# Weights of the experts, projections and feed-forward layers stored in DRAM piece by piece, one 8 KB run a partition

## The chip, the cores and the metric

The kernel runs on one core of a Trainium2 chip. The metric is the device time of one execution in microseconds; the kernel before takes 2042.43 us (median of 3 runs, 2041.69 to 2044.41).

## What is computed

Two blocks of two layers each, over 256 tokens of width 1024, all in f32. Cut to what matters for the weights:

```python
# first block, layer 0 (even mixer) and layer 1 (odd mixer)
mod = silu(c) @ ada_w[layer] + ada_b[layer]              # 1024 x 6144
h = rms_norm(x) * (1 + sc1) + sh1
x = x + g1 * mixer(h, w_in, w_out)                       # 1024 x 3584 or 3072, 1024 x 1024
h = rms_norm(x) * (1 + sc2) + sh2
for e in range(16):                                      # top 2 of 16 experts, from the best of 4 groups
    he = silu(h @ w_gate[e]) * (h @ w_up[e])             # 1024 x 512 each
    y += combine[:, e] * (he @ w_down[e])                # 512 x 1024
x = x + g2 * y
# second block, layer 0 (rwkv) and layer 1 (dilated attention)
x = x + 0.5 * swiglu_ffn(x, pre_w_in, pre_w_out)         # 1024 x 5632, 2816 x 1024
x = x + mixer(rms_norm(x), ...)                          # a_w_in 1024 x 2816, a_w_out; b_w_q, b_w_out, kv_w
x = x + 0.5 * swiglu_ffn(x, post_w_in, post_w_out)
```

Every weight is used once, by all 256 tokens. The experts' weights are 2 x 16 x 3 matrices of 2 MB, 201 MB in all, and are read whole, whatever the router picks.

## The kernel before, in words

Five engines run one program each, written out by hand with semaphores; SP's (`sp`, lines 746 to 810) does little but issue the loads of weights, in the order of the list `PL.pieces` that the class `Plan` (lines 142 to 245) makes before the program is built.

**Pieces.** A piece is 128 partitions x 2048 f32, 8 KB a partition, 1.05 MB. Outside the expert stages the pieces go through `ring`, three slots of one piece; a slot's next load waits for the events in `after`, mostly the split of the piece that it held before. The split makes two parts of each piece, `w_hi` by ScalarE (`split_piece`, L2344) and `w_lo` by VectorE (L3112), and TensorE multiplies by both. `static_piece(n)` issues piece n:
- kind `ada`: layer 0's `ada_w`, 24 pieces, a partition's 8 KB being one run of DRAM already (row `8 p + t` of the matrix), runs 192 KB apart. Unchanged.
- kind `gemm`: a projection, 61 pieces. `(k p) n -> p k n` gives partition p the rows p, 128 + p, ... of the matrix: 8 runs of 1 KB (pieces of 256 columns, 19 of them: `a_in` and the first 4 column groups of `odd_in`) or 4 runs of 2 KB (512 columns, 42).
- kinds `gate`, `up`, `down`: a feed-forward piece, 132 in all. Gate and up are 8 runs of 1 KB, 256 columns wide; down is 2 runs of 4 KB.
- kind `rwkv`: parameters. Unchanged.
- kind `moe`: a whole expert stage, `moe(name, blocks)`.

**The expert stages.** `experts` holds twelve pieces, in three thirds. A stage has 24 passes: 8 of gate (k = rows 128 k to 128 k + 127 of all 16 experts), 8 of up, 8 of down (2 halves of the columns x 4 parts of the rows). A pass is 4 pieces, one for each 4 experts (`load_block(p, g)`, issued at L796): 4 runs of 2 KB a partition, one from each expert. In gate and up weights a run of one partition is followed in memory by that of the next partition; in down weights, which are 4 KB wide, runs of neighbouring partitions lie 4 KB apart. The first twelve pieces are issued as their places come free at the end of the stage before; from pass 3 on a piece waits for `m_base` (TensorE is done with the same piece of three passes before), and the first of a pass also for `m_dve` and `m_act` (the copies are done too).

TensorE (`group(p, g)`, L1616) multiplies for each pass 4 base groups (their own weights from `experts`, one piece each) and 4 further groups, whose 15 tiles VectorE (L3552) and ScalarE (L2550) copy out of `experts` by the router's choice. Between passes stand turned tiles (`turn`, L1623; `slot_weights` and `turned_sel`, L1571 and L1580), the next layer's modulation (L1324, L1328), and the sums over experts (`scatter`, L1631).

**POOL's loads** (`block.gpsimd`) run beside SP's on a queue of their own: at the start the inputs and `mem_w_kv` (`mem_weights`, L837), later layer 1's `ada_w` (`ada_load_pair`, L904, and `ada_load`, L899), which VectorE multiplies and sums (L3240) and TensorE in part (L1490), and small tables. `ada_load_pair` takes two neighbouring parts of a row, 8 KB a partition; `ada_load` one, 4 KB. None of them is changed.

```python
def load_block(p, g):                                    # in moe(name, blocks)
    ...
    at = 512 * (NE * third(layer, p) + 4 * g)
    sp.dma_start(experts[:, at:at + 4 * 512].rearrange("p (e n) -> p e n", e=4), src.rearrange("e p n -> p e n"))\
      .then_inc(sem(pass_landed(layer, p, g)[0]), 16)
```

Of the kernel before, what the change touches and what calls it, by code (L numbers as in the profile page):

```python
# [30 lines left out]
P = 128  # L31
# [3 lines left out]
KD = D // P  # L35
# [4 lines left out]
PIECE = 2048  # L40
# [9 lines left out]
DFF = 2816  # L50
HC = 256
MOE_PASSES = 24
MOE_DEPTH = 3
BASE_GROUPS, GROUPS = 4, 8
# [169 lines left out]
def plan():  # L224
    p = Plan()

    for row in range(KD):
        p.ada(row, 0)
    p.gemm("even_in", EVEN_W, between=EVEN_ADA)
    p.gemm("even_out", D)  # L230
    p.moe("moe0")
    p.gemm("odd_in", ODD_W, feat=range(4))
    p.gemm("odd_out", D)
    p.moe("moe1")
    p.swiglu("pre0", FFN_CHUNKS)
    p.gemm("a_in", A_W, feat=range(5))
    p.rwkv()
    p.gemm("a_out", D)
    p.swiglu("post0", FFN_CHUNKS)
    p.gemm("kv", 1536)  # L240
    p.swiglu("pre1", FFN_CHUNKS)
    p.gemm("b_q", D)
    p.gemm("b_out", D, deep=4)
    p.swiglu("post1", FFN_CHUNKS)
    return p


PL = plan()
STAGES = {**PL.gemms, **PL.swi}

# [52 lines left out]
def build(nc, a, out):  # L303
    ctx = ExitStack()
    with ctx:
        def sb(name, shape, dt=F32):
            return ctx.enter_context(nc.sbuf_tensor(name, shape, dt))
# [3 lines left out]
        def sem(name):  # L311
            if name not in sems:
                sems[name] = ctx.enter_context(nc.semaphore(name))
            return sems[name]
# [15 lines left out]
        x = sb("x", [P, NT, D])  # L330
# [9 lines left out]
        router_w = sb("router_w", [P, KD, NE])  # L340
        router_b = sb("router_b", [P, NE])
        order_i = sb("order_i", [P, OVER_TILES + 1], I32)

        def overlay(name, shape, dt, at):

            return nc.alloc_sbuf_tensor_at(name, shape, dt, offset=at)

        experts = overlay("experts", [P, MOE_DEPTH * NE * 512], F32, pool_at + 4 * (PROJ + 1024))
# [14 lines left out]
        def view(off, *dims):  # L363
            n = int(np.prod(dims))
            v = pool[:, off:off + n]
            if len(dims) == 2:
                return v.rearrange("p (a b) -> p a b", a=dims[0])
            if len(dims) == 3:
                return v.rearrange("p (a b c) -> p a b c", a=dims[0], b=dims[1])
            return v  # L370
# [14 lines left out]
        def piece(n):  # L385

            s = PL.pieces[n]["slot"]
            return ring[:, s * PIECE:(s + 1) * PIECE]
# [122 lines left out]
        def third(layer, p):  # L511
            return (p + 1 - layer) % MOE_DEPTH
# [35 lines left out]
        def kind_of(p):  # L548
            return ("gate", p) if p < 8 else ("up", p - 8) if p < 16 else ("down", p - 16)
# [8 lines left out]
        def pass_landed(layer, p, g):  # L558
            return f"m_landed{p % MOE_DEPTH}{g}", 16 * (MOE_PASSES // MOE_DEPTH * layer + p // MOE_DEPTH + 1)
# [42 lines left out]
        gate = view(HT, NT, 768)  # L602
# [112 lines left out]
        for name, g in PL.gemms.items():  # L715
            for c in range(g["n"]):
                kind = gemm_dst(name, c)[0]
# [28 lines left out]

        @block.sync
        def _(sp):
            def source(kind, name, c):

                layer = int(name[-1])
                w_in = a[f"ffn_{name[:-1]}_w_in_2"][layer].rearrange("(k p) n -> p k n", p=P)
                w_out = a[f"ffn_{name[:-1]}_w_out_2"][layer].rearrange("(k p) n -> p k n", p=P)
                return {"gate": w_in[:, :, HC * c:HC * c + HC], "up": w_in[:, :, DFF + HC * c:DFF + HC * c + HC],
                        "down": w_out[:, 2 * c:2 * c + 2, :]}[kind]

            def load(n, src, k):
                s = PL.pieces[n]["slot"]
                sp.dma_start(piece(n).rearrange("p (k n) -> p k n", k=k), src).then_inc(sem(f"landed{s}"), 16)

            def static_piece(n):
                pc = PL.pieces[n]
                kind, what = pc["kind"], pc["what"]
                for e in pc["after"]:
                    sp.wait_ge(sem(e[0]), e[1])
                if kind == "ada":
                    src = a["ada_w"][0].rearrange("(p t) n -> p (t n)", t=KD)
                    load(n, src[:, what * PIECE:(what + 1) * PIECE].unsqueeze(1), 1)
                elif kind == "gemm":
                    name, o, cols, k0, ks = what  # L770
                    src = {"even_in": a["even_w_in"][0], "even_out": a["even_w_out"][0], "odd_in": a["odd_w_in"][0],
                           "odd_out": a["odd_w_out"][0], "a_in": a["a_w_in_2"][0], "a_out": a["a_w_out_2"][0], "kv": a["kv_w_2"],
                           "b_q": a["b_w_q_2"][0], "b_out": a["b_w_out_2"][0]}[name]
                    load(n, src.rearrange("(k p) n -> p k n", p=P)[:, k0:k0 + ks, o:o + cols], ks)
                elif kind == "rwkv":
                    for o, src in ((3072, a["c_rw_masks"]), (1536, a["a_lnx_g_2"][0].partition_broadcast(P)),
                                   (2304, a["a_lnx_b_2"][0].partition_broadcast(P))):
                        sp.dma_start(rwkv_par[:, o:o + src.shape[1]], src).then_inc(sem("rwkv_in"), 16)
                else:
                    name, c = what  # L780
                    load(n, source(kind, name, c), 2 if kind == "down" else KD)

            def moe(name, blocks):

                layer = int(name[-1])
                def load_block(p, g):

                    kind, k = kind_of(p)
                    es = slice(4 * g, 4 * g + 4)
                    if kind == "down":  # L790
                        h, f = k // 4, k % 4
                        src = a["exp_w_down"][layer, es, P * f:P * f + P, 512 * h:512 * h + 512]
                    else:
                        src = a["exp_w_gate" if kind == "gate" else "exp_w_up"][layer, es, P * k:P * k + P, :]
                    at = 512 * (NE * third(layer, p) + 4 * g)
                    sp.dma_start(experts[:, at:at + 4 * 512].rearrange("p (e n) -> p e n", e=4), src.rearrange("e p n -> p e n"))\  # L796
                      .then_inc(sem(pass_landed(layer, p, g)[0]), 16)

                order = [(p, g) for p in range(MOE_DEPTH) for g in range(BASE_GROUPS)]
                if layer == 0:  # L800
                    order[8:12] = [(2, 3), (2, 0), (2, 1), (2, 2)]
                for p, g in order:
                    block = BASE_GROUPS * third(layer, p) + g
                    if block >= 3:
                        for e in blocks[block - 3]:
                            sp.wait_ge(sem(e[0]), e[1])
                    elif layer == 0:
                        sp.wait_ge(sem("ada1_used"), (12, 14, 16)[block])
                    elif block == 0:
                        sp.wait_ge(sem("sb_pv"), 16)  # L810
                    load_block(p, g)
                for p in range(MOE_DEPTH, MOE_PASSES):
                    n = MOE_PASSES * layer + p
                    for g in range(BASE_GROUPS):
                        sp.wait_ge(sem("m_base"), BASE_GROUPS * (n - MOE_DEPTH) + g + 1)
                        if g == 0:
                            sp.wait_ge(sem("m_dve"), len(DVE_TILES) * (n - MOE_DEPTH + 1))
                            sp.wait_ge(sem("m_act"), len(ACT_TILES) * (n - MOE_DEPTH + 1))
                        load_block(p, g)

            for n, pc in enumerate(PL.pieces):
                if pc["kind"] == "moe":
                    moe(pc["what"], pc["after"])
                else:
                    static_piece(n)
            sp.wait_ge(sem("x_new"), 10)
            sp.dma_start(out.rearrange("a (t p) d -> p (a t) d", p=P), x[:, :, :]).then_inc(sem("stored"), 16)
            sp.wait_ge(sem("stored"), 16)
# [175 lines left out]
        TR_BASE, n = {}, 0  # L1004
# [1868 lines left out]
        def _(dve):  # L2873
# [1061 lines left out]
            swiglu("post1")  # L3935


_WEIGHTS = ["x", "c", "ada_w", "ada_b", "even_w_in", "even_w_out", "odd_w_in", "odd_w_out", "router_w", "exp_w_gate",
            "exp_w_up", "exp_w_down", "mem_2", "ffn_pre_w_in_2", "ffn_pre_w_out_2", "ffn_post_w_in_2",
            "ffn_post_w_out_2", "mem_w_kv_2", "a_w_in_2", "a_w_up_2", "a_a_up_2", "a_g_up_2", "a_w_out_2", "b_w_q_2",  # L3940
            "b_w_out_2", "kv_w_2", "rel_bias_2", "a_lnx_g_2", "a_lnx_b_2", "router_b"]


# [33 lines left out]
```

## Time and profile before

| what | value |
|---|---|
| median of 3 runs | 2042.43 us (2041.69 to 2044.41) |
| profiled execution, first to last instruction | 2041.6 us |
| TensorE, VectorE, ScalarE busy | 1897.6, 1175.1, 943.9 us |
| bytes read from DRAM | 472.17 MB, 232 GB/s over the span |
| first issue of an `experts` load of the first expert stage | 192.6 us |
| last issue of an `experts` load of the second expert stage | 891.4 us |

The profiled execution's own time isn't given apart from its span, which is 0.8 us under the median of the runs.

How to read it: the page cuts the span into 40 slices of 51 us and gives for each the busy share of every engine and of the 16 DMA engines, with the rate in GB/s. A window is the same for any stretch: for each engine the busy time in us with its number of instructions in brackets, then TensorE's granted clock, the DMA engines' share, and GB/s. The share of the DMA engines can pass 1, since one engine's packets overlap a little.

### The profile page before, as it was taken

How to read it: one execution, taken by the hardware profiler on the slowest of the kernel's cores; microseconds unless marked ns; L12 is line 12 of the kernel's file. 1: busy time of each engine (PE TensorE's matmuls, PEld its weight loads, DVE VectorE, ACT ScalarE, POOL GpSimd, SP SyncE). 2: the span in 40 equal slices, each digit the busy share in tenths (PEclk: the TensorE clock that was granted, in tenths of full speed). 3: DMA queues.
4: the chain of work that ended last, by engine and by line, in shares of the span. 5: the costliest groups of instructions: out<-in, count | busy, mean ns of one | idle time of the engine just before them, and what ended most of it. 6: DMA issues, size and time to landing. Idle time of an engine off the chain costs nothing.

```text
span 2041.6 us, 32610 instructions
## 1 busy us (share of the span) xinstructions
PE 1897.6 (93%) x13784; PEld 1381.8 (68%) x13784; DVE 1175.1 (58%) x1636; ACT 943.9 (46%) x1347; POOL 77.4 (4%) x132
## 2 busy tenths in 40 slices
PE   6998988798998988889999998899999999999998
PEld 4787523244976332338888987788887888778887
DVE  5778633444877432447556664665556675636565
ACT  4345445345463543455445733354445444445442
POOL 2031000000010000000000000000000000200000
PEclk9999999989999989899999989999999999999999
DMA  9887999998958899995555410255555555605552
GB/s 357 320 263 264 333 387 386 387 368 292 344 164 318 310 387 387 371 339 196 186 189 178 127 44 4 85 185 188 195 179 175 192 195 186 171 1 191 195 192 104
DMA packets 261218, 476.43 MB, mean 233 GB/s; under 512 B 8513, under 2 KB 118145, under 8 KB 255697
## 3 DMA queue, kind: packets, MB, share of 16 engines
q1 hardware_dynamic: 250960, 431.02, 60.6%
q0 software_dynamic: 10112, 43.32, 6.4%
q8 instruction: 110, 1.80, 0.4%
q14 instruction: 36, 0.29, 0.0%
HBM read 472.17 MB, written 2.14 MB: 232 GB/s over the span
## 4 chain that ended last, share of the span: by engine, by line
PE 73%; DMA 12%; DVE 7%; ACT 5%; issue 2%; SPq 0%; POOL 0%; ACTq 0%; DVEq 0%; POOLq 0%
PE psum L1175 16%; PE psum L1210 11%; PE psum L1616 9%; PE psum L1180 8%; PE psum L1130 6%; DMA experts<-in_exp_w_down 4%; DMA experts<-in_exp_w_up 4%; DMA experts<-in_exp_w_gate 2%; PE psum L1558 1%; PE psum L1344 1%; PE psum L1079 1%; PE psum L1143 1%; PE psum L1145 1%; PE psum L1144 1%; DVE w_lo L3112 1%
## 5 line engine op out<-in xcount | busy, mean ns | idle before, releaser
L3112 DVE TENSOR_TENSOR w_lo<-ring,w_hi 128x2048 fp32r<-128x2048 f32 x191 | 436.0, 2289 | 192.2 <-ACT w_hi L2344 190.4
L2344 ACT ACTIVATE w_hi<-ring 128x2048 fp32r<-128x2048 f32 x191 | 364.7, 1913 | 207.0 <-PE psum L1210 118.1
L1175 PE MATMUL psum<-h_both,w_hi 128*128 128x512 f32 x1408 | 442.6, 395 | 1.9 <-DVE h_both L3894 1.3
L1180 PEld LDWEIGHTS psum<-h_both,w_lo 128*128 128x128 f32 x1408 | 264.5, 188 | 61.8
L2550 ACT ACTIVATE pool<-experts 128x512 f32 x332 | 184.0, 621 | 228.1 <-PE psum L1616 98.0
L3552 DVE COPY pool<-experts 128x512 f32 x380 | 140.9, 423 | 245.2 <-PE psum L1616 115.4
L1180 PE MATMUL psum<-h_both,w_lo 128*128 128x256 f32 x1408 | 277.3, 278 | 0.0
L1175 PEld LDWEIGHTS psum<-h_both,w_hi 128*128 128x128 f32 x1408 | 217.4, 189 | 5.7 <-issue 1.7
L2376 ACT ACTIVATE pool<-psum 128x512 f32<-128x512 f32 x88 | 52.6, 598 | 254.6 <-PE psum L1180 254.5
L1616 PE MATMUL psum<-pool 128*32 128x512 f32 x1008 | 128.4, 626 | 12.5 <-DVE pool L3552 8.5
L1616 PE MATMUL psum<-experts,pool 128*32 128x512 f32 x1024 | 122.3, 607 | 15.7 <-DMA experts<-in_exp_w_down 12.9
L1616 PEld LDWEIGHTS psum<-pool 128*32 128x32 f32 x1008 | 32.6, 112 | 100.9 <-DVE pool L3552 66.3
L1210 PE MATMUL psum<-w_hi,hid_hi 128*128 128x512 f32 x320 | 98.9, 390 | 0.0
L1210 PE MATMUL psum<-w_lo,hid_hi 128*128 128x512 f32 x320 | 98.5, 389 | 0.0
L1210 PE MATMUL psum<-w_hi,hid_lo 128*128 128x512 f32 x320 | 98.5, 389 | 0.0
L1130 PE MATMUL psum<-w_hi,h_both 128*128 128x512 f32 x352 | 98.0, 400 | 0.0
L1616 PEld LDWEIGHTS psum<-experts,pool 128*32 128x32 f32 x1024 | 35.1, 111 | 90.4 <-issue 64.6
L1616 PE MATMUL psum<-experts,xg_high 128*32 128x512 f32 x512 | 63.4, 603 | 23.4 <-DMA experts<-in_exp_w_up 14.9
L1616 PE MATMUL psum<-pool,xg_high 128*32 128x512 f32 x512 | 70.4, 652 | 13.0 <-ACT pool L2550 11.5
L1130 PEld LDWEIGHTS psum<-w_hi,h_both 128*128 128x128 f32 x352 | 65.5, 188 | 17.2 <-issue 4.0
L1143 PE MATMUL psum<-w_hi,h_both 128*128 128x512 f32 x160 | 65.9, 412 | 8.4 <-DVE w_lo L3112 5.7
L3150 DVE TENSOR_TENSOR pool<-pool,psum 128x512 f32<-128x512 f32 x44 | 30.2, 687 | 69.7 <-ACT pool L2376 69.7
(507 smaller groups left out, 2998.6 us busy)
## 6 DMA issues: line engine op xcount, KB each, us to landing
experts<-in_exp_w_gate SPq DMA_DIRECT2D x64, 1024.0 KB, 12.1
experts<-in_exp_w_up SPq DMA_DIRECT2D x64, 1024.0 KB, 14.4
experts<-in_exp_w_down SPq DMA_DIRECT2D x64, 1024.0 KB, 15.0
ring<-in_ffn_pre_w_in SPq DMA_DIRECT2D x44, 1024.0 KB, 5.1
ring<-in_ffn_post_w_in SPq DMA_DIRECT2D x44, 1024.0 KB, 5.2
ring<-in_ada_w SPq DMA_DIRECT2D x24, 1024.0 KB, 7.0
ring<-in_ffn_pre_w_out SPq DMA_DIRECT2D x22, 1024.0 KB, 4.9
ring<-in_ffn_post_w_out SPq DMA_DIRECT2D x22, 1024.0 KB, 4.9
```

The source lines that it names most:

```text
L1130: m = pe.matmul(bank(pair + t)[:, lo:lo + cols], left[:, d, P * t:P * t + P], right[:, k, :], start=first, stop=last)
L1143: pe.matmul(dst, h_hi[:, d, ts], wh[:, k, :], start=d == 0, stop=False)
L1175: pe.matmul(bank(4 + 2 * j + f).rearrange("p (s n) -> p s n", s=2), wh[:, k, P * f:P * f + P], h_both[:, :, k, :], start=k == 0, stop=Fals ...
L1180: return pe.matmul(bank(4 + 2 * j + f)[:, 0:T], wl[:, k, P * f:P * f + P], h_hi[:, k, :], start=False, stop=k == KD - 1, skip_group_check= ...
L1210: m = pe.matmul(bank(2 * t + h), left[:, f, ts], right[:, f, 512 * h:512 * h + 512], start=first, stop=False)
L1616: m = pe.matmul(moe_bank(p, g)[own, :], x_, w, start=first, stop=last)
L2344: act.activation(w_hi[:, (s["split"] + r) % 3, :], piece(s["pieces"][r]), ACT.Copy)\
L2376: act.activation(out_, psum[:, b:b + 2, T:2 * T], ACT.Copy).then_inc(sem("low_moved"), 1)
L2550: act.activation(over_w(layer, p, i), experts[:, bass.ds(tile_at[i // 2] + 512 * NE * third(layer, p), 512)], ACT.Copy)\
L3112: dve.tensor_tensor(w_lo[:, slot, :], piece(s["pieces"][r]), w_hi[:, slot, :].bitcast(F32), ALU.subtract).then_inc(sem("w_lo"), 1)
L3150: dve.tensor_tensor(h, h, psum[:, 4:6, 0:T], ALU.add).then_inc(sem("hid_part"), 1)
L3552: dve.tensor_copy(over_w(layer, p, i), experts[:, bass.ds(tile_at[i // 2] + 512 * NE * third(layer, p), 512)])\
```

## The change

On the host, before the launch, the arrays are put in another order: `weight_pieces` has one 1 MB block for each of the 193 pieces of projections and feed-forward layers, `exp_blocks` one for each of the 192 expert pieces, and in a block the 8 KB of partition 0 come first, then those of partition 1, and so on. The loads read these blocks whole. Order, number and size of the loads, their waits, where they land and everything that the engines compute stay as they are.

```diff
+    p.streamed = [n for n, piece in enumerate(p.pieces) if piece["kind"] in ("gemm", "gate", "up", "down")]
...
-            def load(n, src, k):
+            def load(n, src):
                 s = PL.pieces[n]["slot"]
-                sp.dma_start(piece(n).rearrange("p (k n) -> p k n", k=k), src).then_inc(sem(f"landed{s}"), 16)
+                sp.dma_start(piece(n), src).then_inc(sem(f"landed{s}"), 16)
...
-                    load(n, src[:, what * PIECE:(what + 1) * PIECE].unsqueeze(1), 1)
-                elif kind == "gemm":
-                    name, o, cols, k0, ks = what
...
-                    load(n, src.rearrange("(k p) n -> p k n", p=P)[:, k0:k0 + ks, o:o + cols], ks)
+                    load(n, src[:, what * PIECE:(what + 1) * PIECE])
...
-                    name, c = what
-                    load(n, source(kind, name, c), 2 if kind == "down" else KD)
+                    load(n, a["weight_pieces"][PL.streamed.index(n)])
...
-                    if kind == "down":
-                        h, f = k // 4, k % 4
-                        src = a["exp_w_down"][layer, es, P * f:P * f + P, 512 * h:512 * h + 512]
-                    else:
-                        src = a["exp_w_gate" if kind == "gate" else "exp_w_up"][layer, es, P * k:P * k + P, :]
                     at = 512 * (NE * third(layer, p) + 4 * g)
-                    sp.dma_start(experts[:, at:at + 4 * 512].rearrange("p (e n) -> p e n", e=4), src.rearrange("e p n -> p e n"))\
+                    sp.dma_start(experts[:, at:at + 4 * 512], a["exp_blocks"][layer, p, g])\
                       .then_inc(sem(pass_landed(layer, p, g)[0]), 16)
...
+def expert_blocks(gate, up, down):
+
+    by_row = [w.reshape(2, BASE_GROUPS, 4, KD, P, 512).transpose(0, 3, 1, 4, 2, 5) for w in (gate, up)]
+    by_half = down.reshape(2, BASE_GROUPS, 4, 4, P, 2, 512).transpose(0, 5, 3, 1, 4, 2, 6)
+    return np.concatenate([w.reshape(2, 8, BASE_GROUPS, P, PIECE) for w in (*by_row, by_half)], 1)
+
+
+def weight_pieces(n):
+
...
+        pieces.append(rows.reshape(-1, P, rows.shape[1]).transpose(1, 0, 2).reshape(P, PIECE))
+    return np.stack(pieces)
```

## Rows read from the trace of the kernel before

**Rows 1.** The page: span, busy times, and DMA in 40 slices.

```profile
span 2041.6 us, 32610 instructions
...
PE 1897.6 (93%) x13784; PEld 1381.8 (68%) x13784; DVE 1175.1 (58%) x1636; ACT 943.9 (46%) x1347; POOL 77.4 (4%) x132
...
DMA  9887999998958899995555410255555555605552
GB/s 357 320 263 264 333 387 386 387 368 292 344 164 318 310 387 387 371 339 196 186 189 178 127 44 4 85 185 188 195 179 175 192 195 186 171 1 191 195 192 104
```

**Rows 2.** Window of a feed-forward stage: PE, PEld, DVE, ACT, POOL busy, clock, DMA share, GB/s.

```profile
1000.00:1050.00 50.00, 50.00 (x267) 42.89 (x266) 30.12 (x26) 21.95 (x19) 0.00 (x0) 1.00 0.58 191
```

**Rows 3.** Windows of the first (260 to 490) and second (700 to 910 us) expert stage.

```profile
260.00:400.00 140.00, 114.19 (x928) 36.28 (x920) 44.68 (x117) 58.16 (x106) 0.00 (x0) 0.95 1.05 386
400.00:460.00 60.00, 57.87 (x431) 25.65 (x432) 29.11 (x66) 27.22 (x50) 0.57 (x1) 0.91 1.04 370
460.00:490.00 30.00, 23.48 (x178) 7.36 (x173) 8.22 (x20) 12.50 (x24) 0.00 (x0) 0.94 1.04 369
700.00:820.00 120.00, 99.28 (x808) 33.82 (x804) 39.08 (x104) 52.32 (x95) 0.00 (x0) 0.94 1.05 387
820.00:840.00 20.00, 19.54 (x146) 7.00 (x149) 10.74 (x22) 7.70 (x14) 0.00 (x0) 0.87 1.03 363
840.00:860.00 20.00, 16.69 (x132) 3.96 (x128) 6.61 (x17) 8.95 (x16) 0.00 (x0) 0.91 1.04 370
860.00:880.00 20.00, 19.53 (x136) 8.66 (x132) 13.07 (x27) 11.55 (x22) 0.00 (x0) 1.00 1.05 383
880.00:910.00 30.00, 24.26 (x184) 7.03 (x176) 8.97 (x22) 12.98 (x25) 0.00 (x0) 0.94 1.03 358
```

**Rows 4.** Shorter windows inside the first expert stage.

```profile
290.00:310.00 20.00, 14.11 (x120) 3.38 (x120) 5.22 (x15) 6.30 (x12) 0.00 (x0) 1.00 1.05 386
340.00:350.00 10.00, 9.51 (x93) 3.18 (x86) 2.96 (x8) 3.86 (x7) 0.00 (x0) 1.00 1.05 387
435.00:440.00 5.00, 4.51 (x48) 1.45 (x44) 1.60 (x5) 2.27 (x4) 0.00 (x0) 1.00 0.98 318
```

**Rows 5.** The chain of waits, first expert stage: start us, us, what.

```profile
280.56 27.80 DMA experts<-in_exp_w_gate x2
```

**Rows 6.** The view of DMA: packets, then issues xcount, KB each, median us to landing.

```profile
DMA packets 261218, 476.43 MB, mean 233 GB/s; under 512 B 8513, under 2 KB 118145, under 8 KB 255697
...
ring<-in_ffn_pre_w_in SPq DMA_DIRECT2D x44, 1024.0 KB, 5.1
...
rcols<-in_rwkv_cols POOLq DMA_DIRECT2D x1, 25.0 KB, 30.6
```

**Rows 7.** POOL in order of time: start us, us, line, operation, xcount, idle before.

```profile
5.97 0.55 POOL L845 DMA_DIRECT2D rcols<-in_rwkv_cols  x1
...
186.03 2.09 POOL L904 DMA_DIRECT2D pool<-in_ada_w  x4 [2.89 <-DVE w_lo L3112]
```

**Rows 8.** Windows in which ada_w's 8 KB runs are fetched.

```profile
12.00:20.00 8.00, 2.27 (x5) 1.85 (x6) 4.57 (x6) 2.87 (x7) 0.21 (x1) 1.00 1.02 413
190.00:198.00 8.00, 7.61 (x34) 5.97 (x32) 7.46 (x10) 2.04 (x2) 0.00 (x0) 1.00 1.03 425
```

**Rows 9.** The chain of waits again, before the second expert stage.

```profile
608.82 3.74 DMA pool<-in_ada_w
...
626.50 6.65 DMA pool<-in_ada_w
```

**Rows 10.** TensorE in order of time: start us, us, line, operation, idle before.

```profile
38.34 1.88 PE L1344 MATMUL psum<-pool 128*128 128x512 f32 x4
...
227.07 1.06 PE L1490 MATMUL psum<-pool,cact 128*32 128x512 f32 x8 [0.41 <-DMA pool<-in_ada_w]
...
229.34 3.00 PE L1558 MATMUL psum<-sel,xn_parts 128*128 128x512 f32 x12 [0.57 <-DVE sel L3482]
```

More of the change, by code:

```diff
@@ L748, in _ @@
         def _(sp):
[L749 to L755, printed above, removed]
-            def load(n, src, k):
+            def load(n, src):
                 s = PL.pieces[n]["slot"]
-                sp.dma_start(piece(n).rearrange("p (k n) -> p k n", k=k), src).then_inc(sem(f"landed{s}"), 16)
+                sp.dma_start(piece(n), src).then_inc(sem(f"landed{s}"), 16)
             def static_piece(n):
@@ L767, in static_piece @@
                     src = a["ada_w"][0].rearrange("(p t) n -> p (t n)", t=KD)
-                    load(n, src[:, what * PIECE:(what + 1) * PIECE].unsqueeze(1), 1)
-                elif kind == "gemm":
-                    name, o, cols, k0, ks = what
-                    src = {"even_in": a["even_w_in"][0], "even_out": a["even_w_out"][0], "odd_in": a["odd_w_in"][0],
-                           "odd_out": a["odd_w_out"][0], "a_in": a["a_w_in_2"][0], "a_out": a["a_w_out_2"][0], "kv": a["kv_w_2"],
-                           "b_q": a["b_w_q_2"][0], "b_out": a["b_w_out_2"][0]}[name]
-                    load(n, src.rearrange("(k p) n -> p k n", p=P)[:, k0:k0 + ks, o:o + cols], ks)
+                    load(n, src[:, what * PIECE:(what + 1) * PIECE])
                 elif kind == "rwkv":
@@ L786, in load_block @@
                 def load_block(p, g):
-                    kind, k = kind_of(p)
-                    es = slice(4 * g, 4 * g + 4)
-                    if kind == "down":
-                        h, f = k // 4, k % 4
-                        src = a["exp_w_down"][layer, es, P * f:P * f + P, 512 * h:512 * h + 512]
-                    else:
-                        src = a["exp_w_gate" if kind == "gate" else "exp_w_up"][layer, es, P * k:P * k + P, :]
                     at = 512 * (NE * third(layer, p) + 4 * g)
-                    sp.dma_start(experts[:, at:at + 4 * 512].rearrange("p (e n) -> p e n", e=4), src.rearrange("e p n -> p e n"))\
+                    sp.dma_start(experts[:, at:at + 4 * 512], a["exp_blocks"][layer, p, g])\
                       .then_inc(sem(pass_landed(layer, p, g)[0]), 16)
@@ L3935, in _ @@
             swiglu("post1")
[L3938 to L3941, printed above, removed]
+def expert_blocks(gate, up, down):
[3 more added lines that the diff above has]
+def weight_pieces(n):
+    dense = {"even_in": n["even_w_in"][0], "even_out": n["even_w_out"][0], "odd_in": n["odd_w_in"][0], "odd_out": n["odd_w_out"][0],
+             "a_in": n["a_w_in_2"][0], "a_out": n["a_w_out_2"][0], "kv": n["kv_w_2"], "b_q": n["b_w_q_2"][0], "b_out": n["b_w_out_2"][0]}
+    pieces = []
+    for at in PL.streamed:
+        kind, what = PL.pieces[at]["kind"], PL.pieces[at]["what"]
+        if kind == "gemm":
+            name, o, cols, k0, ks = what
+            rows = dense[name][P * k0:P * (k0 + ks), o:o + cols]
+        else:
+            stage, c = what
+            layer, part = int(stage[-1]), f"ffn_{stage[:-1]}_w"
+            o = HC * c + (DFF if kind == "up" else 0)
+            rows = n[f"{part}_out_2"][layer][HC * c:HC * c + HC] if kind == "down" else n[f"{part}_in_2"][layer][:, o:o + HC]
+        pieces.append(rows.reshape(-1, P, rows.shape[1]).transpose(1, 0, 2).reshape(P, PIECE))
+    return np.stack(pieces)
+_WEIGHTS = ["x", "c", "ada_w", "ada_b", "router_w", "mem_2", "mem_w_kv_2", "a_w_up_2", "a_a_up_2", "a_g_up_2", "rel_bias_2",
+            "a_lnx_g_2", "a_lnx_b_2", "router_b"]
 def kernel(**inputs):
@@ L3967 @@
     arrays["rel_t"] = np.ascontiguousarray(np.concatenate([rel, np.zeros((256 - rel.shape[0], 8), rel.dtype)], 0))
+    arrays["weight_pieces"] = weight_pieces(n)
+    arrays["exp_blocks"] = expert_blocks(n["exp_w_gate"], n["exp_w_up"], n["exp_w_down"])
     arrays.update(constants())
```

## The prediction

> **What bounds the kernel now.** I read the page's slices first [rows 1]: TensorE is busy 93% of the span, and the DMA engines are full in two stretches only, slices 6 to 10 and 14 to 18, where they move up to 387 GB/s. These are the two expert stages. Next come windows. In a feed-forward stage [rows 2] TensorE is busy 50.00 of 50 us and DMA moves 191 GB/s; three feed-forward windows I read were alike to 2 GB/s. No faster transfer helps there. In the expert stages [rows 3] it is the other way round: DMA share 1.05, 386 and 387 GB/s over 140 and 120 us, while TensorE is busy 114.19 and 99.28 us. Inside them two kinds of window alternate [rows 4]: at 340 us TensorE is fed (9.51 of 10, 93 matmuls), at 290 us it starves (14.11 of 20, 120 matmuls). The chain of waits says the same: from 280.56 us it stands for 27.80 us in transfers of gate weights [rows 5]. A pass of 16 experts is 4 pieces of 1.05 MB, 10.8 us at 387 GB/s. Twelve pieces fit in the ring, some 32 us of transfer, so TensorE's side work (turns, sums) doesn't stop the stream. In the first two thirds of each stage the transfers alone set the pace.
>
> **What the change alters.** The same bytes go over the same queues into the same places, after the same waits. Only the runs in DRAM differ: 192 expert pieces in 2 KB runs, 132 feed-forward pieces (88 in 1 KB, 44 in 4 KB) and 61 of projections (19 in 1 KB, 42 in 2 KB) all become 128 runs of 8 KB. That is 240,640 packets replaced by 49,280; of the 261,218 packets of [rows 6] some 69,900 should be left. No engine gains or loses an instruction, and SP issues as many transfers.
>
> **The rate of 8 KB runs** isn't shown for these weights, but the stream has others. From 190 to 198 us POOL's four `ada_w` loads (8 KB a partition, [rows 7]) are nearly alone in the engines and go at 425 GB/s [rows 8]; from 12 to 20 us SP's `ada_w` pieces of 8 KB, mixed with POOL's small loads, go at 413. The bounds are 387 (nothing gained) and 425. I take 425: it is the row with least else in it, and a share of 1.03 beside 1.05 says that both are the engines at full work. A piece then takes 2.47 instead of 2.71 us.
>
> A rule speaks against this. The Trainium skill, page "DMA: Bandwidth & Descriptors", Specifications, gives 512 B as the smallest transfer for line rate; by it runs of 2 KB are there already and the sum is 0. The rows of 387 and 425 GB/s don't agree with it. The same page, "Why small descriptors are slow", gives some 3 cycles for each packet, 67 for 2 KB against 64 of data; an estimate from that is 3.4% for the expert stages, a third of what the rows show.
>
> **First two thirds of the expert stages.** 140 us at 386 GB/s are 54.0 MB, at 425 GB/s 127.2 us: 12.8 us saved. 120 us at 387 are 46.4 MB, 109.3 us: 10.7 saved. Ends: 413 GB/s saves 9.2 and 7.6.
>
> **The down thirds** (400 to 490, 820 to 910 us) need two sums [rows 3].
> - DMA: 33.3 and 33.1 MB. At 387 they would take 86.0 and 85.4 us, at 425 78.3 and 77.8: 7.7 and 7.6 saved by the rate. The rows take 90, since they hold short dips, as 318 GB/s at 435 us [rows 4], eight in all over both stages, and in down weights only. Down weights are the only expert loads whose 2 KB runs lie 4 KB apart, so the dips may well go with the layout: then 11.7 and 12.2 are saved.
> - TensorE: it can't go faster than fed. By busy time (81.35 us at 9.51 per 10) it needs 85.5 of the 90 us, and 84.1 in the second stage: caps of 4.5 and 5.9. By matmuls (93 per 10 us fed, 178 in the 30 starved us of the first stage; 132 and 184 in 50 us of the second) the caps are 10.9 and 16.0. A starved group's last matmul counts its whole length as busy, so the first pair is too low.
>
> The rate terms lie between the caps, and I take them. What the dips give back above that meets TensorE, which is what is late next. Sum of the four: 12.8 + 10.7 + 7.7 + 7.6 = 38.8 us.
>
> **Where the long packets cost.** SP's weights share the 16 engines with POOL's loads. If the queues take turns by packet, a POOL packet waits behind 8 KB instead of 2 KB. The nearest price: two equal loads of `ada_w` took 3.74 us alone and 6.65 beside SP's experts [rows 9]. The later one (512 KB, 8 packets an engine) gets 6 KB × 8 × 16 = 0.79 MB more in front, 1.85 us, and stands on the chain. At 227.07 us TensorE waits 0.41 us for a 1 MB `ada_w` load (again 8 packets an engine, 1.85 us), and had 0.57 us of slack behind it [rows 10]: 1.3 us. At the start the second half of `mem_w_kv` is in before `rcols`, which lands at 5.97 + 30.6 = 36.6 us [rows 6, 7], and TensorE reads it at 38.34 [rows 10]; SP has two pieces queued, and if both go in front, not only one's worth, that is 1.05 MB or 2.5 us more, so 39.1: 0.8 us late. Together 4.0 us, between 0 (SP has nothing queued) and 8. The Trainium skill, the same page, "Queues, rings and completion order", has the queues taking turns at packets; no row here shows the order of packets.
>
> **Costed at nothing.** The feed-forward and projection pieces: a 1 MB piece in 1 KB runs lands 5.1 us after its issue, and 191 GB/s are one piece of 1.05 MB every 5.5 us, by TensorE's pace and not by the transfers' [rows 2, 6], and if TensorE were not full, a piece would still gain only the few tenths between 2.5 us at 425 and its present transfer time. SP's issuing: behind the ring of three slots.
>
> **Sum.** The profiled execution spans 2041.6 us, 0.8 below the median 2042.43 of the runs. 2041.6 - 38.8 + 4.0 = 2006.8 us, and with the 0.8 around it 2007.6 us.
>
> **Rivals.**
> - *Packets cost less than the rows say* (the rate of 425 is partly POOL's queue or those addresses). At 400 GB/s the 166.8 MB of both stages save by rate 431.4 - 417.0 = 14.4 us (431.4 being the four rate-bound times at 386 and 387), less 4.0: 2032 us. For it: no 8 KB row is wholly alone. Against: 413 GB/s even when mixed. 5%. The skill's estimate above would end here.
> - *The engines are at their ceiling already* (share 1.05, TensorE 93% busy): only the turns cost, 2042.4 to 2046.4. Against it is the 425. 4%, half of it within 0.2%. The skill's 512 B rule ends here.
> - *Slower: lock step in memory.* Place: the expert stream. A piece is now one block of 1 MB in which the engines' runs lie at equal power-of-two distances; today's `ada_w` runs lie 192 KB apart and show no such block. The dips to 318 GB/s prove that addresses can slow the stream. Price: at 350 GB/s the 166.8 MB take 476.6 instead of 440 us (both stages whole), and 4.0 more: 2083 us. It decides from below 383 GB/s (166.8 MB in 436 us). Against: gate and up runs are adjacent already, without a dip. 3%. The skill's same page, "Latency and other measured facts", tells of such slowing for row pitches of 512 KiB and more, and recommends contiguous tiles; its pitches are not met here.
> - *The change doesn't do what it says*: if the engines cut 8 KB runs at 2 KB, packets stay at 261,000 and the time at 2042.4. Against: `ada_w` runs now. 2%.
>
> **How the numbers follow.** 0.2% (4.1 us) is what can be told from no change. My forecast has 86%. Low end: 425, dips gone, no cap, no turns lost: 2042.4 - 47.4 = 1995.0. High end: 413 with 9.2 + 7.6 + 4.5 + 5.3 = 26.6 saved and 4.0 lost: 2019.8, rounded to 2020. Nothing further is needed to leave out less than 2 in 10. Faster: 86 + 5 = 91%. Same: 2 + 2 = 4%. Slower: 2 + 3 = 5%.
>
> **What the profile after would show.** Packets near 69,900; windows of both expert stages at 420 to 425 GB/s until the down passes; the gap from the first to the last `experts` transfer shorter by 18 to 21 us in each stage; down passes with TensorE fed most of the time; feed-forward windows still at 50.00 of 50; the `ada_w` load near 626 us at 8 us or more. I am wrong if those windows stay at 387, if the dips grow, or if the chain shows a POOL transfer of over 10 us.

## The result, and the profile after

The changed kernel takes 2007.24 us (median of 4 runs, 2004.27 to 2009.94) against 2042.97 us of the kernel before in the same comparison: a ratio of 0.9824, 95% interval 0.9809 to 0.9839. The forecast was 2007.6 us, between 1995.0 and 2020. The profiled execution spans 2006.9 us, 34.7 less than the one before.

The page of the kernel after (lines as in [rows 1], and the packets of [rows 6]):

```profile
span 2006.9 us, 32610 instructions
...
PE 1879.5 (94%) x13784; PEld 1385.4 (69%) x13784; DVE 1175.4 (59%) x1636; ACT 943.7 (47%) x1347; POOL 77.6 (4%) x132
...
DMA  9885999997957799975555210345545555505552
GB/s 355 310 290 215 353 393 392 421 420 289 347 161 312 301 421 420 421 294 210 190 193 181 86 43 4 148 169 189 190 174 190 189 191 189 151 21 190 189 189 105
DMA packets 69857, 476.43 MB, mean 237 GB/s; under 512 B 8512, under 2 KB 8576, under 8 KB 15056
```

The same bytes, the same instructions, 69,857 packets instead of 261,218, and 421 GB/s where 387 stood. Windows of the kernel after, first in the gate and down passes of the first stage, one in the down passes of the second, then a feed-forward stage (columns as in [rows 2]):

```profile
280.00:290.00 10.00, 9.51 (x92) 3.24 (x88) 3.00 (x9) 3.84 (x8) 0.00 (x0) 1.00 1.02 421
430.00:440.00 10.00, 8.93 (x68) 3.90 (x64) 4.82 (x11) 5.42 (x10) 0.00 (x0) 1.00 1.01 421
850.00:860.00 10.00, 9.54 (x89) 3.05 (x92) 6.12 (x15) 6.62 (x14) 0.00 (x0) 1.00 1.01 415
1000.00:1050.00 50.00, 50.00 (x267) 42.90 (x266) 30.17 (x25) 21.71 (x18) 0.00 (x0) 1.00 0.54 190
```

The expert stream is faster in gate, up and down weights alike and has lost its dips; the feed-forward stage is as it was [rows 2], down to the number of matmuls.

To follow the time, I cut both executions at marks that the chain of waits has in every kernel: the start of the gather that opens an expert stage, the start of the last group of sums that closes it, and the feed-forward pieces. The chain of the kernel before, then of the kernel after (start us, us, what; x14 closes a stage, x32 opens the second; the first opens at 229.34 us before [rows 10]):

```profile
496.54 3.43 PE psum L1631 x14
...
658.61 7.52 PE psum L1558 x32
...
915.48 3.41 PE psum L1631 x14
```

```profile
5.19 34.32 DMA pool<-in_mem_w_kv
39.55 1.98 PE psum L1323 x4
...
221.96 10.39 DMA pool<-in_ada_w
234.09 14.54 PE psum L1537 x64
...
483.49 3.41 PE psum L1610 x14
...
613.48 8.01 DMA pool<-in_ada_w
...
648.17 9.14 PE psum L1537 x32
...
886.54 3.41 PE psum L1610 x14
```

The expert stages went from 267.2 to 249.4 us and from 256.9 to 238.4 us: 36.3 us saved. The rest nearly cancels: the start up to the first gather is 4.75 us longer, the stretch between the stages 2.6 us longer (162.1 to 164.7), and the rwkv stage, in which hardly a weight is loaded, 7.2 us shorter. Three of the forecast's places of cost are in the chain by name: POOL's `mem_w_kv`, and two `ada_w` loads.

### The profile page after: what moved, and what is told of

Same layout as the page of the kernel before. It is cut to its first block, busy times and chain, and to the rows that moved or that the text cites. A ratio compares the mean times of both kernels' runs of the same rounds, so it can differ in the third digit from the quotient of the medians.

```text
span 2006.9 us, 32610 instructions
## 1 busy us (share of the span) xinstructions
PE 1879.5 (94%) x13784; PEld 1385.4 (69%) x13784; DVE 1175.4 (59%) x1636; ACT 943.7 (47%) x1347; POOL 77.6 (4%) x132
## 2 busy tenths in 40 slices
DMA packets 69857, 476.43 MB, mean 237 GB/s; under 512 B 8512, under 2 KB 8576, under 8 KB 15056
## 4 chain that ended last, share of the span: by engine, by line
PE 75%; DMA 10%; DVE 7%; ACT 5%; issue 2%; SPq 0%; POOL 0%; DVEq 0%; ACTq 0%; POOLq 0%
PE psum L1154 16%; PE psum L1189 11%; PE psum L1595 10%; PE psum L1159 8%; DMA experts<-in_exp_blocks 7%; PE psum L1109 6%; DMA pool<-in_mem_w_kv 2%; PE psum L1537 2%; PE psum L1122 1%; PE psum L1610 1%; PE psum L1123 1%; PE psum L1124 1%; PE psum L1323 1%; DMA pool<-in_ada_w 1%; DVE w_lo L3091 1%
## 5 line engine op out<-in xcount | busy, mean ns | idle before, releaser
L1595 PE MATMUL psum<-pool 128*32 128x512 f32 x1008 | 123.1, 603 | 12.9 <-DVE pool L3531 10.9
L1595 PE MATMUL psum<-pool,xg_high 128*32 128x512 f32 x512 | 65.2, 612 | 13.9 <-ACT pool L2529 10.4
## 6 DMA issues: line engine op xcount, KB each, us to landing
pool<-in_mem_w_kv POOLq DMA_DIRECT2D x4, 1024.0 KB, 16.6
```

The source lines that it names most:

```text
L1595: m = pe.matmul(moe_bank(p, g)[own, :], x_, w, start=first, stop=last)
```

## The experiments

Eight more kernels ran, and the changed one once more (after_again). The medians are over all runs of a kernel, and the ratios against the kernel before run beside it; the stage lengths, between the marks above, are those of one profiled execution each:

| kernel | median us | first stage | between | second stage | rwkv |
|---|---|---|---|---|---|
| before | 2042.4 | 267.2 | 162.1 | 256.9 | 270.1 |
| after | 2007.2 | 249.4 | 164.7 | 238.4 | 262.9 |
| experts_only | 2006.2 | 249.2 | 164.6 | 238.4 | 265.0 |
| pieces_only | 2043.7 | 267.1 | 161.9 | 257.2 | 267.1 |
| blocks_2k | 2038.4 | 264.8 | 161.9 | 254.8 | 267.0 |
| blocks_4k | 2018.2 | 253.4 | 162.8 | 243.3 | 263.6 |
| down_old | 2023.9 | 256.5 | 164.7 | 248.4 | 262.3 |
| after_again | 2005.9 | 248.3 | 163.4 | 236.8 | 261.4 |
| short_beside | 2001.2 | 249.1 | 160.3 | 237.1 | 262.6 |
| mem_8k | 2007.3 | 245.5 | 163.1 | 236.8 | 262.5 |
| short_and_mem | 2002.4 | 250.1 | 162.0 | 240.1 | 266.9 |

My theory was that the length of the runs sets the rate of the expert stream, and nothing else of the change matters but the turns beside POOL. The rivals: that the projections' and feed-forward pieces have a part, that one contiguous block is what helps, and that the down thirds are TensorE's.

**experts_only.** The kernel before, with the new `load_block` and `exp_blocks` alone:

```diff
-                    sp.dma_start(experts[:, at:at + 4 * 512].rearrange("p (e n) -> p e n", e=4), src.rearrange("e p n -> p e n"))\
+                    sp.dma_start(experts[:, at:at + 4 * 512], a["exp_blocks"][layer, p, g])\
```

> Only the experts' loads take the new layout, projections and feed-forward pieces stay as before. Run-length theory (the expert stream is the whole gain, SP's long runs beside POOL's loads are the cost): both expert stages save the 36 us that the trace of after shows, the 3 us lost at the start of the kernel are not lost, the loss before the first expert stage (ada_w load) and before the second stays: 2042.5 - 36 + 4 = about 2010, and 2006 if the rwkv stage runs at full clock as it did after. Rival (the short runs of the projections matter too): slower than after by over 5 us.

Measured: 2006.23 us (ratio 0.9812, 0.9783 to 0.9841), stages of 249.2 and 238.4 us, where about 2010 or 2006 us was expected. The experts are the whole gain. The other half of the change is worth nothing that can be seen in the time. Of the loss at the start most is avoided: TensorE reads `mem_w_kv` without a wait at 37.48 us.

**pieces_only.** The other half alone: the new `weight_pieces`, the old `load_block`.

```diff
-                    load(n, src.rearrange("(k p) n -> p k n", p=P)[:, k0:k0 + ks, o:o + cols], ks)
+                    load(n, a["weight_pieces"][PL.streamed.index(n)])
```

> Only projections and feed-forward pieces take the new layout, the experts stay in 2 KB runs. Run-length theory: nothing gained where TensorE is full, 3 us lost at the start (second half of mem_w_kv later than TensorE wants it), expert windows stay at 387 GB/s: 2043 to 2047 us. Rival (the pieces bring part of the gain): below 2038 us.

Measured: 2043.67 us, ratio 1.0013 (1.0000 to 1.0026), stages as before. 193 pieces in 128 packets instead of 256 to 1024 bring nothing. Its first gather opens at 233.3 us, 4.0 later than before. Its chain doesn't show `mem_w_kv`, but TensorE's rows in order of time do: TensorE starts on it at 39.13 instead of 38.34 us [rows 10], after a wait. The chain goes by another of POOL's loads, `router_w`, and by the weight piece that comes late behind it:

```profile
39.13 1.98 PE L1330 MATMUL psum<-pool 128*128 128x512 f32 x4 [0.40 <-DMA pool<-in_mem_w_kv]
```

```profile
8.47 34.49 DMA router_w<-in_router_w
...
60.69 8.52 DMA ring<-in_weight_pieces
```

So the trace shows the expected loss at the start, 2.9 us of it by the first VectorE step of the mixer's heads (L3218 before, 170.88 us; 173.81 here). The last 1.0 of the 4.0 comes behind it, where the clock was lower (0.73 from 176 to 186 us, before 0.83). The ratio of 1.0013 is too near to 1 to show it as a time.

**blocks_2k.** As after, but a block is stored as four arrays of 128 x 2 KB, and read so:

```diff
-                    sp.dma_start(experts[:, at:at + 4 * 512], a["exp_blocks"][layer, p, g])\
+                    sp.dma_start(experts[:, at:at + 4 * 512].rearrange("p (c n) -> p c n", c=4),
+                                 a["exp_blocks"][layer, p, g].rearrange("c p n -> p c n"))\
```

> As after, but each expert block of 1 MB is stored as 4 x 128 runs of 2 KB and fetched so: one contiguous block, short runs. Run-length theory: expert windows back at 387 GB/s, but no dips in the down passes; first two thirds of both stages as before, some 4 to 8 us gained in the down thirds, ada_w loads not slowed: 2035 to 2043 us. Rival (that a piece is one block of memory is what speeds the stream): windows at 420 GB/s, about 2007 us.

Measured: 2038.43 us, ratio 0.9976 (0.9964 to 0.9989). Its windows in gate and down passes:

```profile
280.00:290.00 10.00, 8.25 (x76) 2.12 (x67) 2.96 (x8) 3.86 (x7) 0.00 (x0) 1.00 1.05 386
430.00:440.00 10.00, 9.50 (x92) 3.04 (x84) 3.52 (x10) 4.34 (x8) 0.00 (x0) 1.00 1.05 386
850.00:860.00 10.00, 7.23 (x60) 1.63 (x56) 3.58 (x9) 4.85 (x9) 0.00 (x0) 1.00 1.06 387
```

One block of memory, and still 386 and 387 GB/s: the rival falls. But the dips are gone, and 2.4 and 2.1 us of the stages with them. So the change has two effects that the forecast named, and this kernel has one alone: contiguity removes the dips, run length sets the rate. A run is as long in SBUF as in DRAM in all these kernels; on which of the two sides its length counts isn't shown.

**blocks_4k.** The same with two arrays of 128 x 4 KB (`c=2`).

> As after, but each expert block of 1 MB is stored as 2 x 128 runs of 4 KB and fetched so. If every packet costs the same over its bytes, the rows of 2 KB (387 GB/s, 512 packets a piece) and 8 KB (420, 128 packets) give 9 ns a packet on each engine, and runs of 4 KB (256 packets) go at 408 to 410 GB/s; the expert stages take 255 and 244 us, a third of the gain of 8 KB over 2 KB still missing: 2015 to 2020 us. Rival (engines cut at 4 KB, or only 8 KB runs are fast): 420 or 387 GB/s.

Measured: 2018.21 us (0.9890, 0.9865 to 0.9916), stages of 253.4 and 243.3 us. Its windows, gate and down:

```profile
260.00:310.00 50.00, 42.90 (x372) 12.56 (x376) 17.09 (x46) 21.77 (x41) 0.00 (x0) 1.00 1.03 409
...
400.00:450.00 50.00, 48.34 (x363) 22.26 (x363) 22.82 (x51) 24.27 (x45) 0.00 (x0) 0.93 1.03 409
```

409 GB/s where 408 to 410 was expected from the rows at 2 and 8 KB. A piece of 1.05 MB takes 2.71, 2.56 and 2.49 us in runs of 2, 4 and 8 KB, with 32, 16 and 8 packets on each engine: 9 ns a packet in both steps (0.15 us for 16, 0.07 for 8). So the three rates fit one cost for each packet; by this estimate 8 packets of 8 KB still carry 0.07 us. What the 9 ns are spent on isn't shown.

**down_old.** As after, but down weights by the old layout.

```diff
+                    if kind == "down":
+                        h, f, es = k // 4, k % 4, slice(4 * g, 4 * g + 4)
+                        src = a["exp_w_down"][layer, es, P * f:P * f + P, 512 * h:512 * h + 512]
+                        sp.dma_start(experts[:, at:at + 4 * 512].rearrange("p (e n) -> p e n", e=4), src.rearrange("e p n -> p e n"))\
...
+                    else:
```

> As after, but the down weights keep the old layout (2 KB runs, 4 KB apart). Theory: the down thirds run at 387 GB/s with dips to 320 again; TensorE is what limits much of that stretch, so 8 to 16 us are lost against after: 2015 to 2023 us. Rival (TensorE alone bounds the down thirds, the transfers there are worth nothing): within 4 us of after.

Measured: 2023.87 us (0.9911, 0.9887 to 0.9935), 16.6 above after by the medians and 17.6 above experts_only, which ran beside it, a little more than I expected. Its windows in gate and down passes:

```profile
280.00:290.00 10.00, 9.02 (x88) 2.71 (x83) 4.48 (x12) 5.54 (x10) 0.00 (x0) 1.00 1.01 422
...
400.00:410.00 10.00, 10.00 (x76) 6.27 (x72) 1.73 (x7) 1.29 (x3) 0.00 (x0) 0.81 1.01 349
410.00:420.00 10.00, 9.49 (x76) 2.38 (x72) 4.17 (x12) 5.23 (x10) 0.00 (x0) 0.85 1.05 388
420.00:430.00 10.00, 9.51 (x92) 3.34 (x88) 3.05 (x8) 3.87 (x8) 0.00 (x0) 1.00 1.03 334
```

The same kernel has 422 GB/s for gate weights, and for down weights the old rate of 388 with the old dips, to 334. The down thirds are worth 7.1 and 10.0 us (256.5 - 249.4, 248.4 - 238.4), so TensorE doesn't bound them alone; the other two thirds 10.7 and 8.5 us.

**after_again, short_beside, mem_8k, short_and_mem** ran side by side, for the costs beside POOL's loads. `short_beside` fetches in 2 KB runs what is fetched beside POOL: three `even_in` pieces and the first twelve of each expert stage.

```diff
+                    if i < 3:
+                        sp.dma_start(piece(n).rearrange("p (c n) -> p c n", c=4), a["pieces_first"][i].rearrange("c p n -> p c n"))\
...
+                    if p < MOE_DEPTH:
+                        sp.dma_start(experts[:, at:at + 4 * 512].rearrange("p (c n) -> p c n", c=4),
+                                     a["exp_first"][layer, p, g].rearrange("c p n -> p c n"))\
```

`mem_8k` leaves SP alone and gives POOL's load 8 KB runs; `short_and_mem` has this and the second half of the diff above.

```diff
-                src = a["mem_w_kv_2"][layer].rearrange("(k p) n -> p k n", p=P)[:, 4 * half:4 * half + 4, :]
-                pl.dma_start(mem_w[layer][half], src)
+                pl.dma_start(mem_w[layer][half].rearrange("p k n -> p (k n)"), a["mem_blocks"][layer, half])
```

> The changed kernel itself, once more, for comparison with the three kernels beside it on the same chip: 2004 to 2010 us. The rwkv stage (last ffn piece of one to first of the next) took 270.1 us before and 262.9 after; if that is TensorE's granted clock and not the layout, it will come out anywhere from 262 to 270 here.

> As after, but the pieces that are fetched beside POOL's loads, the first three of even_in and the first twelve of each expert stage, are fetched in 2 KB runs (from blocks of 1 MB still); the rest in 8 KB runs. Theory (long runs of SP hold up POOL's loads): the stretch from the end of the first expert stage to the gather of the second falls from 164.7 to 162 us, the last ada_w load before it from 8.0 to 6.6 us, the gather of the first stage starts 1 to 2 us earlier, both stages keep their 249 and 238 us: 3 to 5 us less than after_again. Rival (the lost us have another cause, such as the earlier end of the first stage): the stretch stays at 164.7.

> As after, and POOL's mem_w_kv loads get the same treatment: one run of 8 KB a partition, so that POOL's turns are as long as SP's. Theory: the second half of mem_w_kv lands before TensorE wants it (by 37 us instead of 39.5), 1 us gained at the start and nothing elsewhere: within 2 us of after_again. Rival (POOL's loads at the start are short of something else than turns): landing unchanged.

> The first twelve pieces of each expert stage in 2 KB runs, mem_w_kv in 8 KB runs, all else as after. Theory: the sum of both, 3 to 5 us less than after_again, and the fastest of the four: 2001 to 2005 us.

Measured, five runs each: 2005.94 (0.9821, 0.9798 to 0.9845), 2001.17 (0.9803, 0.9785 to 0.9821), 2007.28 (0.9828, 0.9805 to 0.9850) and 2002.36 us (0.9794, 0.9775 to 0.9812). The chain of after_again, then of short_beside:

```profile
5.21 33.73 DMA pool<-in_mem_w_kv
...
221.55 10.45 DMA pool<-in_ada_w
...
611.91 8.14 DMA pool<-in_ada_w
```

```profile
607.78 6.56 DMA pool<-in_ada_w
```

With short runs beside them POOL's loads are as fast as before (6.56 against 6.65 us in [rows 9]), and the `mem_w_kv` wait and the first `ada_w` wait have left the chain. The gather opens at 228.7 instead of 233.7 us and the stretch between the stages is 3.1 us shorter. Not all of these 8.1 us belong to the loads. Of the 5.0, 0.9 lie between 171 and 219 us, where TensorE had a higher clock (1.00 against 0.87 from 176 to 186 us). Of the 3.1, 1.5 lie between the last `ada_w` load and the gather, where the other kernels with short runs there took as long as after_again (25.3 to 25.5 us). The stages keep their length, so the long runs aren't missed in the first twelve pieces.

The last `ada_w` load before the second stage follows the runs of SP's pieces beside it in every trace: 6.56 to 6.65 us beside 2 KB (five kernels), 7.96 to 8.43 beside 8 KB (five), and in blocks_4k between them:

```profile
615.31 7.38 DMA pool<-in_ada_w
```

That confirms that long runs of SP hold up POOL's loads. In what order the engines serve the two queues isn't shown, and the step from 2 to 4 KB is 0.8 us and that from 4 to 8 KB 0.6 to 1.0, not twice as long, as it would be if POOL's wait grew with SP's bytes alone. The gain as a time, 4.8 us by the medians, is likely but not shown: the intervals of the ratios overlap. short_and_mem, which I had expected to be the fastest, can't be told from short_beside (1.2 us slower by the medians, 0.9794 against 0.9803 by the ratios). Its profiled execution was its slowest run (2009.56 us), and its stage lengths, of which two are over the others', shouldn't be read as the median's. In mem_8k POOL's queue is faster, by the view of DMA of after_again and of mem_8k:

```profile
rcols<-in_rwkv_cols POOLq DMA_DIRECT2D x1, 25.0 KB, 33.7
```

```profile
rcols<-in_rwkv_cols POOLq DMA_DIRECT2D x1, 25.0 KB, 29.9
```

The table, `rcols`, is issued at 5.53 us (5.98 in after_again), so it lands at 35.4 instead of 39.7, and the wait for `mem_w_kv` has left the chain. But the kernel isn't faster for it by the medians (2007.28 against 2005.94 us).

## Why the prediction was right, step by step

- **TensorE bounds the feed-forward stages, the transfers the expert stages.** Right: 190 GB/s and 50.00 of 50 after, 421 GB/s in the stages, and pieces_only at 1.0013.
- **The rate, 425.** Nearly: 421, 34 GB/s over 387 for the 38 of the forecast. The row of 425 at 190 us was a short one, 8 us; 413 from the mixed row was too low. The three rates of 2, 4 and 8 KB don't agree with the rule of 512 B in the Trainium skill (page "DMA: Bandwidth & Descriptors", Specifications), by which there would have been no gain. Nor do they agree with the forecast's estimate of 3.4% from the 3 cycles a packet of the Trainium skill (same page, "Why small descriptors are slow"): 421 against 387 is 8.8%.
- **First two thirds, 12.8 and 10.7.** Measured by down_old against before: 10.7 and 8.5. The forecast has 2.1 and 2.2 us too much. At 421 GB/s the same working gives 11.6 and 9.7, so about half of it is the rate; the other 0.9 and 1.2 us stay open.
- **Down thirds, 7.7 and 7.6.** Measured by after against down_old: 7.1 and 10.0. In the first stage of after the stream fell for a while (last section); short_beside, after_again and mem_8k against down_old give 7.4, 8.2 and 11.0 there and 11.3 to 11.6 in the second. So the second term was taken too low, and the first lies at the low end of what was measured. The rate alone gives 6.9 and 6.9 at 421 GB/s; blocks_2k shows that the dips are worth 2.4 and 2.1. I had guessed that what the dips give back would be lost on TensorE. It wasn't, or not in all: the caps by busy time (4.5 and 5.9) are passed in both stages, those by matmuls (10.9 and 16.0) are not passed by more than 0.1 in any run.
- **Sum of the stages, 38.8.** Measured 36.3 (17.8 and 18.5).
- **Long packets beside POOL, 0.8 + 1.3 + 1.85 = 4.0.** The places are right, the first term is too small. At the start TensorE reads `mem_w_kv` at 39.55 instead of 38.50 us, 1.05 late, for 0.8. But by the VectorE step of 170.88 us the kernel is 2.98 late, and the layout has a part in the rest too. The six kernels with projections in 8 KB runs beside the old `mem_w_kv` (after, after_again, pieces_only, blocks_2k, blocks_4k, down_old) are 1.5 to 3.4 us late there, each after a wait of 0.40 to 1.34 us for `mem_w_kv`. The four others (experts_only, short_beside, mem_8k, short_and_mem) are 0.1 to 0.8 late, without that wait. How much of it is `router_w` and the piece behind it, as in pieces_only, and how much a lower clock (0.76 from 40 to 54 us after, 0.88 before) stays open. From the router's start to the gather (the ScalarE step at 215.19, after 219.21) it is 14.88 to 15.13 us in the five kernels that fetch the first expert pieces in 8 KB runs and 14.14 to 14.17 in the other six: 0.7 to 1.0, for 1.3. The last `ada_w` load takes 8.01 us instead of 6.65, 1.36 for 1.85, and every other trace agrees. Together 2.98 + 0.73 + 1.36 = 5.1 us, for 4.0. short_beside takes most of them away.
- **What the sum didn't have.** 1.0 us more before the first gather, where the clock was lower (0.73 from 176 to 186 us, before 0.83). 1.2 more between the last `ada_w` load and the second gather, again at a lower clock (0.76 from 621 to 635 us after, 0.86 from 633 to 645 before); after_again and mem_8k don't have them (25.4 and 25.2 us, before 25.5, after 26.7). And 5.8 less after the second stage (rwkv 7.2 less, the dilated stage 1.4 more). Hardly any of these 5.8 can come from the layout: in the rwkv stage the chain waits for one weight piece, 5.24 us before and 4.90 after. Saved 36.3 and 5.8, lost 5.1, 1.0 and 1.2: 34.8, and 34.7 measured. That the forecast of 2006.8 for the span met 2006.9 is luck in part: the stages gave 2.5 us less than the sum said, the long packets cost 1.1 more, and the stretches that it didn't have gave 3.6. Over five runs after_again spreads from 1998.9 to 2009.6.
- **The rivals.** Cheap packets (2032 us), a ceiling already reached, lock step in memory and packets cut at 2 KB are all out by the 421 GB/s and the 69,857 packets. The dips had a cause in the layout, as the third said, but in the old one.

## What to carry to other kernels

Where a stream of weights keeps the DMA engines at a share of 1, count its packets: here each cost 9 ns on its engine, and runs of 8 KB for 2 KB gave 8.8% on the stream and 36.3 us on its two stages. Where the compute engine is full, the same edit is worth nothing, and beside another queue's loads on the critical path it costs (8.0 instead of 6.6 us for one of them): there short runs may serve better, which the chain of short_beside shows and its time doesn't yet. A change of layout should be costed by stage, by which wait ends last in each.

## What I had not expected

The kernel's own spread goes with TensorE's granted clock: in the five runs of after_again the mean clock rises from 0.983 in the slowest (2009.6 us) to 0.992 in the fastest (1998.9). The rwkv stage took 261.4 to 270.1 us in eleven traces. Before, TensorE was granted 0.92 in a window of 60 us of it (1150 to 1210), after 1.00 throughout. The three longest are those of the kernels with all experts in 2 KB runs (before, pieces_only, blocks_2k), short_and_mem just behind them; why isn't shown. And in an expert stage a low clock reaches the transfers. Windows of the kernel after, then of after_again, at the side work that follows the eighth pass:

```profile
320.00:330.00 10.00, 9.25 (x44) 8.85 (x43) 2.27 (x6) 1.91 (x4) 0.00 (x0) 0.50 1.01 419
330.00:340.00 10.00, 9.42 (x68) 2.75 (x72) 3.64 (x11) 5.90 (x12) 0.00 (x0) 0.79 0.72 283
```

```profile
320.00:330.00 10.00, 9.12 (x68) 5.39 (x68) 4.29 (x11) 5.92 (x12) 0.00 (x0) 0.84 1.01 419
330.00:340.00 10.00, 9.06 (x88) 3.20 (x88) 4.54 (x13) 5.51 (x11) 0.00 (x0) 1.00 1.01 419
```

In the first TensorE ran at the lower of its two levels, 1.2 GHz, through the whole window from 320 us, after it had been busy for 6.66 of 10 us, starved for weights: 44 matmuls instead of 68. The twelve places of `experts` filled, and the stream fell to 283 GB/s for 10 us, which is 3.3 us of transfer at 421. In the forecast I had said that side work doesn't stop the stream. At 387 GB/s it hardly did even at the low clock, as pieces_only shows:

```profile
320.00:330.00 10.00, 10.00 (x54) 8.36 (x47) 0.87 (x3) 0.14 (x1) 0.00 (x0) 0.53 1.05 386
330.00:340.00 10.00, 9.12 (x56) 4.04 (x58) 2.72 (x6) 5.18 (x11) 0.00 (x0) 0.61 1.05 387
340.00:350.00 10.00, 9.05 (x84) 2.88 (x80) 4.58 (x12) 5.53 (x10) 0.00 (x0) 1.00 1.04 377
```

At the same place and a clock of 0.50, 4 KB runs fall to 329 GB/s (blocks_4k) and 8 KB runs to 283, 274 and 261 (after, experts_only, short_and_mem); at 0.84 and more they keep 419. That fits a faster stream that fills the twelve places sooner. What it costs a stage is less clear: the three stages with the fall took 249.4, 249.2 and 250.1 us, after_again, short_beside and mem_8k without it 248.3, 249.1 and 245.5. Nor is it shown what decides the clock: mem_8k was busy for 6.81 of the 10 us before, hardly more than after, and was granted 0.91.
